# A two-layer hybrid decoder step on one core: a new deal of the adaLN pieces, and a start by feature tile

## The chip, the cores and the metric

The kernel runs on one core of a Trainium2 chip. The metric is device time in microseconds (us): the median of repeated executions of the whole step, both layers, from one launch. Lower is better. Engines are named as in the profile: PE (TensorE, matrix multiplication), PEld (its weight loads), DVE (VectorE), ACT (ScalarE), POOL (GpSimd), SP (SyncE, which issues nearly all transfers).

## The reference, cut to what matters

Two layers, each of three sub-layers: SwiGLU FFN, token mixer, SwiGLU FFN. 256 prompt tokens and 8 sequences of 8 sampled tokens (320 columns in all) go through together; D_MODEL is 1024, D_FF 2816, everything is float32. Each sub-layer is wrapped in a norm before, a norm after and a shift, scale and gate that come from one vector per sequence:

```
mod = (silu(c) @ ada_w + ada_b).reshape(B, 3, 3, 1024)      # per layer: 9 chunks of 1024 columns

def modulate(y, i): return rms_norm(y, g_pre[i]) * (1.0 + mod[:, i, 1]) + mod[:, i, 0]
def residual(y, out, i, w): return y + w * mod[:, i, 2] * rms_norm(out, g_post[i])

x = residual(x, swiglu(modulate(x, 0), f_in[0], f_out[0]), 0, 0.5)
x = residual(x, mixer(modulate(x, 1), ...), 1, 1.0)
x = residual(x, swiglu(modulate(x, 2), f_in[1], f_out[1]), 2, 0.5)
```

The mixer is one input projection, then a gated linear recurrence (HGRN2), sliding-window attention with sinks and a short convolution side by side, and one output projection. The nine vectors of conditioning are 1 prompt and 8 samples. `ada_w` is 2 layers x 1024 x 9216 floats, 75 MB: a third of all weights.

## The kernel before, in words

**Layout.** Activations lie feature-first: `x`, `y`, `sq` are 8 feature tiles of 128 partitions x 320 columns. A weight unit of 1 MB (1.4 MB for an FFN's second matrix) lands in one of two slots of `raw`. ACT copies it, rounded, to `WHI` (L899), DVE writes the rest, raw minus WHI, to `WLO` (L1180). The normed input is split in the same way into `hmh` and `hml`. A product is three matmuls (mm3, L466 to L468), so a *pair* of 256 output features takes 2 x 8 x 3 = 48 matmuls. An iteration of FFN-in is two pairs: slot 0 makes the gate (PSUM banks 0 and 1), slot 1 the other half (banks 2 and 3). FFN-in has 11 iterations, FFN-out 4 (banks 4 and 5, then 0 and 1), the mixer's input projection 5, its output projection 2.

**The adaLN product** is cut into 72 pieces of 1 MB: 18 chunks (shift, scale or gate of one sub-layer) of 4 pieces. A piece is 128 partitions x 2048 floats; PE multiplies it in `columns` (L475, 8 matmuls of 256 columns, which the trace counts as 16). When a chunk's four pieces are summed in its PSUM bank (6 or 7), ACT copies the bank to `adp` (`ada_copy`, L904), PE turns it (`turned`, L492) and DVE adds the bias (`mod_out`, L1195). The first two chunks, shift and scale of the first norm, come before all else, in buffers `first` (L214); the other 64 pieces are dealt out by the list `HOMES` to places in PE's program, and each has a *home*: the tile `ada`, or a part of `stage`, which lies over the normed operands and the FFN's intermediate (homes S, B, C), over `z` and `big` of the mixer (P), or over the idle normed operands (M). A home is loaded again only when its last piece has been multiplied: SP waits for `s_part` in `piece` (L364).

**What sets the order.** Everything is written out by hand; each engine runs its own list and waits on semaphores. PE takes one piece per iteration of the first FFN-in. A norm gap (`gap`, L590) is: statistics of the sub-layer's output (`y_stats`, L528 and L530), five pieces, statistics of the new x (`x_stats`, L522), three pieces, and then the first pair of the next sub-layer with k outside, as the feature tiles of the normed input come. Meanwhile ACT and DVE do: reciprocal root, y scaled and added to x, x squared (L924), reciprocal root, `x_norm` (DVE L1221 and L1242, ACT L935 and L938). In the mixer, PE runs six Gram groups (L655, each in one of two bank pairs), and DVE masks (L1409) and sums (L1413) each; DVE then scales the states (L1428), scores come (L684), and the recurrence's output (L700, L703) needs the states. Layer 0 has 12 pieces in its mixer, layer 1 has 8: one after each Gram group, and the rest between later steps.

**At the start**, SP issues small inputs, x, seven pieces, waits for a home and issues the eighth, then two weight units. PE does x_stats, the eight pieces and the turns; DVE then makes the whole scale (L1211) and the norm runs over the tiles, while PE multiplies the first pair with k outside and the second with k inside.

**The states' and caches' outputs** leave in ten transfers that ACT issues between the mixer and its output projection (L1130 to L1140).

Of the kernel before, what the change touches and what calls it, by code (L numbers as in the profile page):

```python
# [16 lines left out]
F32 = mybir.dt.float32  # L17
# [36 lines left out]
START = 2  # L54
# [3 lines left out]
FFN_GAP = ["S0", "S1", "ada", "B0", "B1", "B2", "C0", "C1"]  # L58
MIX_GAP = ["ada", "M"]
OUT_GAP = ["P0", "P1", "P2", "ada", "S0", "S1", "P0", "ada"]  # L60
N_FIRST, N_MIX = 12, (12, 8)
HOMES = ["ada"] * N_FIRST + FFN_GAP + MIX_GAP * 6 + OUT_GAP + FFN_GAP + FFN_GAP + MIX_GAP * 4
LANDS = 12
# [5 lines left out]
         "C0": (HHL0 + 7040, HHL0 + 8064), "C1": (HHL0 + 9088, HHL0 + 10112),  # L69
         "P0": (Z0 + 2240, Z0 + 3264), "P1": (Z0 + 4288, Z0 + 5312), "P2": (BIG0, BIG0 + 1024)}  # L70
# [30 lines left out]
DVE_CHAIN = 57  # L101
# [50 lines left out]
def trunk(nc, A, O):  # L152

    ctx = ExitStack()
    with ctx:
# [35 lines left out]
        with ExitStack() as stage_scope:  # L191
# [22 lines left out]
                 yf[:, 0:2048], ada[:, :, :].rearrange("p a b -> p (a b)"), zfl[:, 0:2048]]  # L214
# [32 lines left out]
        def chunk_of(n, j):  # L247

            return START + 3 * n + j

# [10 lines left out]
        s_first = [sem(f"s_first{i}") for i in range(START * PIECES)]  # L261
# [5 lines left out]
        s_part = sem("s_part")  # L267
        s_adp = sem("s_adp")
# [44 lines left out]
        ADA = A["ada_w"].rearrange("l u p n -> (l u) p n")  # L313
# [35 lines left out]
        def _(sp):  # L349
# [5 lines left out]
            for u in range(START * PIECES):  # L355
                if u == START * PIECES - 1:
                    sp.wait_ge(s_part, 2)
                sp.dma_start(first[u], ADA[((DEPTH - 1) * CHUNKS + 7) * PIECES + u]).then_inc(s_first[u], 16)

            taken = {"ada": 6}  # L360

            def piece(p):

                u = START * PIECES + p  # L364
                if HOMES[p] in taken:
                    sp.wait_ge(s_part, taken[HOMES[p]] + 2)
                taken[HOMES[p]] = u
# [8 lines left out]

            def ffn_in(l, f, off):
# [4 lines left out]
                both(0)  # L382
                n = 3 * l + 2 * f
                if n == 0:
                    piece(0)
                    for it in range(1, IT_IN):
                        piece(it)
                        both(it)
                    piece(N_FIRST - 1)
                else:  # L390
                    if n == 2:
                        sp.wait_ge(s_used[1], l * ITS + OFF_MO + IT_MO + 1)
                        for p in range(36, 40):
                            piece(p)
                    if n == 3:
                        last = (l - 1) * ITS + OFF_F1O + IT_OUT - 1
                        free_ffn(last, 40)
# [4 lines left out]
            def free_ffn(last, p0):  # L402
# [5 lines left out]
                piece(p0 + 6)  # L408
                piece(p0 + 7)
# [10 lines left out]
            for l in range(DEPTH):  # L420
                ffn_in(l, 0, OFF_F0I)
                gap = 12 if l == 0 else 48
                ffn_out(l, 0, OFF_F0O, gap)
                for it in range(IT_MI):
                    for slot in (0, 1):
                        weights(l * ITS + OFF_MI + it, slot, MIN_[l * 2 * IT_MI + it * 2 + slot], W_IN)
                    if it == 0:
                        free_ffn(l * ITS + OFF_F0O + IT_OUT - 1, gap)

                        sp.wait_ge(s_part, START * PIECES + gap + 9)  # L430
# [3 lines left out]
                mix = gap + 8  # L434
                for it in range(IT_MO):
                    for slot in (0, 1):
                        weights(l * ITS + OFF_MO + it, slot, MOUT[l * 2 * IT_MO + it * 2 + slot], W_IN)
                    if it == 0:
                        piece(mix)
                        sp.wait_ge(s_used[1], l * ITS + OFF_MI + IT_MI + 1)  # L440
                        for p in range(mix + 1, mix + 4):
                            piece(p)
                for p in range(mix + 4, mix + N_MIX[l]):
                    piece(p)
                if l == 0:

                    sp.wait_ge(ev["mixl"], 4 * (l + 1))
                    for p in range(32, 36):
                        piece(p)
                ffn_in(l, 1, OFF_F1I)  # L450
                ffn_out(l, 1, OFF_F1O, 40 if l == 0 else None)
# [8 lines left out]
        def _(pe):  # L460
# [18 lines left out]
            def partial(p):  # L479

                u = START * PIECES + p
                c = u // PIECES
# [1313 lines left out]
```

## Time and profile before

| | us |
|---|---|
| median of 3 runs | 1445.57 (1443.24 to 1445.70) |
| profiled execution | 1445.13 |
| its span, first to last instruction | 1443.3 |
| PE busy | 1347.7 (93%) |
| DVE busy | 689.8 (48%) |
| ACT busy | 558.2 (39%) |
| POOL busy | 86.4 (6%) |
| read from HBM | 249.26 MB, 176 GB/s over the span |
| mean granted TensorE clock | 0.972 |

The 1.8 us between the profiled execution's time and its span lie outside the instructions. PE is busy for 1347.7 of 1443.3 us, so what is left to win on waits is under 96 us; the profile's second part shows where PE is not at nine or ten tenths: in the first slice, and in three groups of slices, about 280 to 320 us, 380 to 510 us and 1080 to 1200 us. These are the start, the norm gaps and the two mixers.

### The profile page before, as it was taken

Reading aid. Unit: us, or ns where it says so; the run is one execution under the profiler, and the core shown is the slowest. Engines: PE = TensorE matmul, PEld = TensorE weight load, DVE = VectorE, ACT = ScalarE, POOL = GpSimd, SP = SyncE. Lnnn points to the kernel's source line nnn. Section 1 sums busy time; section 2 is a strip of 40 time slices with the busy share of each in tenths; the row PEclk is TensorE's granted clock in tenths of the full one; section 3 lists DMA queues with packets and bytes.
Section 4 is the critical chain, followed back from the end, with each engine's and each line's share of the span. In section 5 each row is a group of like instructions: output and inputs, shape, how many; then the busy total and the mean of one; then the engine's idle time right before and its main releaser. Section 6 shows DMA issues by size and latency. Waiting matters only on the chain.

```text
span 1443.3 us, 23409 instructions
## 1 busy us (share of the span) xinstructions
PE 1347.7 (93%) x10190; PEld 1256.6 (87%) x10190; DVE 689.8 (48%) x715; ACT 558.2 (39%) x703; POOL 86.4 (6%) x93
## 2 busy tenths in 40 slices
PE   4899999999877999999999999999996888999997
PEld 2799999979744889999989999997994678999997
DVE  0534443358644544444344444435686545444433
ACT  2533343354313553333345333425351445333331
POOL 0000000001611000000000000000035100000000
PEclk9899999999979999999999999999999899999999
DMA  9655656454652744446462344745547042444440
GB/s 362 241 205 203 210 204 246 160 219 146 229 210 94 264 159 147 145 146 248 162 251 99 146 148 151 272 156 196 190 157 264 3 136 88 151 150 163 163 161 37
DMA packets 50372, 255.42 MB, mean 177 GB/s; under 512 B 7022, under 2 KB 12014, under 8 KB 30062
## 3 DMA queue, kind: packets, MB, share of 16 engines
q1 hardware_dynamic: 45872, 249.51, 47.5%
q10 hardware_dynamic: 4238, 3.58, 0.8%
q8 instruction: 67, 1.10, 0.3%
q0 software_dynamic: 176, 1.09, 0.2%
q14 instruction: 19, 0.16, 0.0%
HBM read 249.26 MB, written 4.89 MB: 176 GB/s over the span
## 4 chain that ended last, share of the span: by engine, by line
PE 84%; ACT 6%; DMA 5%; DVE 3%; ACTq 1%; issue 1%; SPq 0%; DVEq 0%
PE PS L466 25%; PE PS L467 25%; PE PS L468 25%; DMA ada<-in_ada_w 3%; PE PS L475 3%; PE PS L522 2%; ACT hmh L935 2%; ACT sq L935 2%; DMA raw<-in_w_in 1%; DMA x<-in_x 1%; PE PS L716 0%; ACT big L1043 0%; PE PS L700 0%; PE PS L616 0%; PE PS L789 0%
## 5 line engine op out<-in xcount | busy, mean ns | idle before, releaser
L466 PE MATMUL PS<-hmh,WHI 128*128 128x320 f32 x1856 | 578.9, 312 | 12.9 <-DVE hml L1242 11.8
L467 PE MATMUL PS<-hml,WHI 128*128 128x320 f32 x1856 | 572.9, 309 | 0.0
L468 PE MATMUL PS<-hmh,WLO 128*128 128x320 f32 x1856 | 572.7, 309 | 0.0
L1180 DVE TENSOR_TENSOR WLO<-raw,WHI 128x2048 fp32r<-128x2048 f32 (+1 forms) x148 | 366.2, 2474 | 390.1 <-ACT WHI L899 390.1
L899 ACT ACTIVATE WHI<-raw 128x2048 fp32r<-128x2048 f32 (+1 forms) x148 | 303.9, 2053 | 346.2 <-PE PS L468 346.1
L466 PEld LDWEIGHTS PS<-hmh,WHI 128*128 128x128 f32 x1856 | 349.4, 188 | 26.1 <-issue 14.7
L467 PEld LDWEIGHTS PS<-hml,WHI 128*128 128x128 f32 x1856 | 349.6, 188 | 0.2
L468 PEld LDWEIGHTS PS<-hmh,WLO 128*128 128x128 f32 x1856 | 349.4, 188 | 0.0
L466 PE MATMUL PS<-hhl,WHI 128*128 128x320 f32 x704 | 216.8, 308 | 0.0
L468 PE MATMUL PS<-hhl,WLO 128*128 128x320 f32 x704 | 216.7, 308 | 0.0
L467 PE MATMUL PS<-hhl,WHI 128*128 128x320 f32 x704 | 216.7, 308 | 0.0
L467 PEld LDWEIGHTS PS<-hhl,WHI 128*128 128x128 f32 x704 | 132.0, 188 | 0.0
L466 PEld LDWEIGHTS PS<-hhl,WHI 128*128 128x128 f32 x704 | 132.0, 188 | 0.0
L468 PEld LDWEIGHTS PS<-hhl,WLO 128*128 128x128 f32 x704 | 132.0, 188 | 0.0
L973 ACT ACTIVATE y<-PS 128x640 f32<-128x640 f32 x44 | 31.0, 705 | 182.7 <-PE PS L468 182.7
L1297 DVE TENSOR_TENSOR y<-y,PS 128x640 f32<-128x640 f32 x44 | 36.1, 821 | 106.1 <-PE PS L468 106.1
L475 PE MATMUL PS<-ada,cT 128*32 128x256 f32 x448 | 34.4, 430 | 28.6 <-DMA ada<-in_ada_w 28.6
L954 ACT ACTIVATE sq<-PS 128x640 f32<-128x640 f32 x18 | 12.7, 705 | 101.7 <-PE PS L468 101.7
L1285 DVE TENSOR_TENSOR acc<-acc,sq 128x320 f32<-128x320 f32 x18 | 8.9, 494 | 83.3 <-ACT sq L954 66.7
L475 PEld LDWEIGHTS PS<-ada,cT 128*32 128x32 f32 x448 | 13.4, 117 | 40.1 <-issue 20.7
L522 PE MATMUL PS<-sq,cst 128*128 128x320 f32 x96 | 32.3, 493 | 15.3 <-ACT sq L1085 11.1
L475 PE MATMUL PS<-stage,cT 128*32 128x256 f32 x592 | 37.9, 392 | 7.5 <-DMA stage<-in_ada_w 7.4
(227 smaller groups left out, 879.7 us busy)
## 6 DMA issues: line engine op xcount, KB each, us to landing
raw<-in_w_in SPq DMA_DIRECT2D x88, 1024.0 KB, 4.7
raw<-in_w_out SPq DMA_DIRECT2D x32, 1408.0 KB, 6.0
stage<-in_ada_w SPq DMA_DIRECT2D x74, 512.0 KB, 6.8
ada<-in_ada_w SPq DMA_DIRECT2D x54, 512.0 KB, 6.0
raw<-in_m_in SPq DMA_DIRECT2D x20, 1024.0 KB, 4.8
raw<-in_m_out SPq DMA_DIRECT2D x8, 1024.0 KB, 6.5
z<-in_ada_w SPq DMA_DIRECT2D x4, 1024.0 KB, 11.9
big<-in_ada_w SPq DMA_DIRECT2D x2, 1024.0 KB, 15.8
```

The costliest lines, as they stand in the source:

```text
L466: mm(out, hi, rhi, start=first, stop=False)
L467: mm(out, hi, rlo, start=False, stop=False)
L468: return mm(out, lo, rhi, start=False, stop=last)
L475: last = mm(PS[32 * j:32 * j + 32, bank, 0:256], cT[:, k, :], halves[i][:, j * 256:(j + 1) * 256], start=(k == 0), stop=(k == KT - 1))
L522: last = mm(PS[:, 5, 0:T], ones, sq[:, k, :], start=(k == 0), stop=(k == KT - 1))
L899: a_(WHI[:, slot, 0:width], raw[:, slot, 0:width], ACT.Copy).then_inc(s_hi[slot], 1)
L935: a_(out[:, k, 0:TP], sq[:, k, 0:TP], ACT.Identity, bias=mod[m][:, 8 + k, 0:1], scale=mod[m][:, 16 + k, 0:1])
L954: a_(sq[:, 0:2, :], PS[:, bank:bank + 2, 0:T], ACT.Square).then_inc(s_sqd, 1)
L973: a_(sg, PS[:, 0:2, 0:T], ACT.Silu).then_inc(s_gread, 1)
L1180: tt(WLO[:, slot, 0:width], raw[:, slot, 0:width], WHI[:, slot, 0:width].bitcast(F32), ALU.subtract).then_inc(s_lo[slot], 1)
L1285: ch.link(tt(acc[:], acc[:], sq[:, 0, :], ALU.add))
L1297: tt(hf, sg, PS[:, 2:4, 0:T], ALU.mult).then_inc(s_uread, 1)
```

## The change: what it does

1. **The deal.** Of the 64 pieces that are dealt, twelve still go to the first FFN-in (two ahead of its second iteration, and then one each). Each of the four full norm gaps takes ten instead of eight: seven between `y_stats` and `x_stats` instead of five, and three behind as before. Each mixer takes six, instead of twelve and eight: one ahead, one after Gram groups 2, 4 and 6, and one at each of two later places. New homes are C2 and P3.
2. **Banks.** Chunks lie in bank 4, 6 or 7 by the table `BANKS`. So that bank 4 and 5 are free, FFN-out uses banks 0 to 3 (its first iteration waits for `s_gread`, its second for `s_uread`), and all `y_stats` go to bank 5. One more wait (`s_mod`) stands ahead of a turn in the mixer's input projection.
3. **The start.** The first shift and scale are laid out anew on the host (`ada0`): a piece holds all 1024 inputs for one feature tile's 128 shifts and 128 scales. PE makes one feature tile's shift and scale from one piece; ACT copies, PE turns by two small matmuls (9 columns each), DVE adds the bias, makes the scale, and the norm of that feature tile follows. Both first pairs run with k outside. SP issues the eight pieces without a wait, with the first two weight units behind pieces 0 and 1.
4. **Outputs.** The ten output transfers of a layer are issued by SP, ahead of the second FFN's weights, and no longer by ACT.
5. **Norms.** In `x_norm` of DVE the two small operations on a tile's samples now follow one another with a link between them, instead of being interleaved over two tiles; and one turn moves from the output projection's first to its second iteration.

```diff
-FFN_GAP = ["S0", "S1", "ada", "B0", "B1", "B2", "C0", "C1"]
-OUT_GAP = ["P0", "P1", "P2", "ada", "S0", "S1", "P0", "ada"]
-N_FIRST, N_MIX = 12, (12, 8)
+FFN_GAP = ["S0", "S1", "ada", "B0", "B1", "B2", "C0", "C1", "C2", "ada"]
+MIX_GAP = ["ada", "M"] * 3
+OUT_GAP = ["P0", "P1", "P2", "P3", "ada", "S0", "S1", "P0", "P1", "ada"]
...
+            taken = {}
+            for k in range(KT):
+                sp.dma_start(first[k], A["ada0"][k]).then_inc(s_first[k], 16)
+                if k < 2:
+                    weights(0, k, WIN_[k], W_IN)
...
                 y_stats(n, 5)
-                for i in range(5):
+                for i in range(7):
                     partial(p + i)
                 x_stats(n + 1)
-                for i in range(5, 8):
+                for i in range(7, 10):
                     partial(p + i)
...
                         last.then_inc(ev["gr"], 1)
                         n += 1
-                        partial(p + n)
+                        if n % 2 == 0:
+                            partial(p + n // 2)
...
+            for k in range(KT):                       # PE
+                pe.wait_ge(s_first[k], 16)
+                if k > 1:
+                    pe.wait_ge(s_m0, k - 1)
...
+                last.then_inc(s_p0, 1)
+                if k:
+                    started(0, k - 1)
+                pe.wait_ge(s_a0, k + 1)
...
+                last.then_inc(s_t0, 1)
+                if k > 2:
+                    started(1, k - 3)
+            started(0, KT - 1)
+            for k in range(KT - 3, KT):
+                started(1, k)
...
+            for k in range(KT):                       # ACT
+                act.wait_ge(s_p0, k + 1)
+                if k > 1:
+                    act.wait_ge(s_t0, k - 1)
+                a_(adps[k % 2], PS[:, 6 + k % 2, 0:256], ACT.Copy).then_inc(s_a0, 1)
+                act.wait_ge(s_mt, k + 1)
+                act.wait_ge(s_m0, k + 1)
+                feed(k, 2, k, k + 1)
+                if k < 2:
+                    hi_split(k, 0, W_IN)
...
+                for k in range(KT):                   # DVE, first_norm; all eight normed(k) stand ahead
+                    dve.wait_ge(s_t0, k + 1)
...
+                        ALU.add, ALU.mult).then_inc(s_m0, 1)
+                    dve.wait_ge(s_m0, k + 1)
+                    shifted(k, 2, k, k + 1)
+                    low(k, k, k + 1)
+                    if k < 2:
+                        lo_split(k, 0, W_IN)
```

`started(slot, k)` is the six matmuls of tile k of a pair; for k = 0 it also waits for both halves of that slot's weights. `feed` is the loop body of ACT's old `x_norm`. The `#` remarks behind loops are added here.

**PE at the start.** Before: x_stats, eight pieces (x24 is three of them, x16 two), the two turns (L492), piece 0 of the deal (`ada`), and the first pair.

```order
L522 MATMUL PS<-sq,cst 128x320 x8
L475 MATMUL PS<-z,cT 32x256 x24
L475 MATMUL PS<-big,cT 32x256 x16
L492 MATMUL PS<-cst,adp 128x128 x2
L475 MATMUL PS<-y,cT 32x256 x8
L475 MATMUL PS<-ada,cT 32x256 x8
L475 MATMUL PS<-z,cT 32x256 x8
L492 MATMUL PS<-cst,y 128x128 x2
L475 MATMUL PS<-ada,cT 32x256 x8
L466 MATMUL PS<-hmh,WHI 128x320
```

And now, where L852 is a piece, L859 the turn of one tile and L492 to L494 the three matmuls of a product:

```order
L547 MATMUL PS<-sq,cst 128x320 x8
L852 MATMUL PS<-z,cT 32x256 x8
L859 MATMUL PS<-cst,adp 128x9 x2
L852 MATMUL PS<-z,cT 32x256 x8
L492 MATMUL PS<-hmh,WHI 128x320
L493 MATMUL PS<-hml,WHI 128x320
L494 MATMUL PS<-hmh,WLO 128x320
L492 MATMUL PS<-hmh,WHI 128x320
L493 MATMUL PS<-hml,WHI 128x320
L494 MATMUL PS<-hmh,WLO 128x320
L859 MATMUL PS<-cst,y 128x9 x2
L852 MATMUL PS<-z,cT 32x256 x8
```

The first products now stand behind two pieces instead of nine, but the second turn stands behind the first tile's six matmuls.

**PE in layer 0's mixer.** Before, from the second Gram group (L655) on, with a piece (L475) behind each group and L668 the states:

```order
L655 MATMUL PS<-big 64x64 x12
L475 MATMUL PS<-ada,cT 32x256 x8
L668 MATMUL PS<-sq 128x128 x8
L655 MATMUL PS<-big 64x64 x6
L655 MATMUL PS<-z,y 64x64 x2
L475 MATMUL PS<-stage,cT 32x256 x8
L655 MATMUL PS<-big 64x64 x12
L655 MATMUL PS<-z,y 64x64 x4
L655 MATMUL PS<-big 64x64 x12
L475 MATMUL PS<-ada,cT 32x256 x8
```

Now, with L680 for the Gram groups, L501 for a piece and L694 for the states:

```order
L680 MATMUL PS<-big 64x64 x12
L501 MATMUL PS<-stage,cT 32x256 x8
L694 MATMUL PS<-sq 128x128 x8
L680 MATMUL PS<-big 64x64 x6
L680 MATMUL PS<-z,y 64x64 x2
L680 MATMUL PS<-big 64x64 x12
L680 MATMUL PS<-z,y 64x64 x4
L680 MATMUL PS<-big 64x64 x12
L501 MATMUL PS<-ada,cT 32x256 x8
```

Behind the states three Gram groups now follow one another up to the next piece. The homes alternate, so a home comes up again four groups after its last use; before, it was two.

## Rows read from the trace of the kernel before

**Rows 1.** Busy time by stretch (both mixers' Gram parts, both output projections):

```profile
382.76:422.81 40.05, 24.38 (x429) 14.67 (x425) 22.06 (x39) 4.34 (x6) 15.38 (x18) 0.79 0.85 307
1086.01:1116.72 30.71, 18.66 (x396) 12.73 (x393) 20.68 (x38) 4.35 (x6) 15.36 (x18) 0.89 0.83 309
459.21:493.42 34.21, 30.47 (x199) 30.21 (x198) 11.64 (x16) 12.24 (x23) 1.23 (x3) 0.95 0.69 238
1152.29:1181.89 29.60, 28.71 (x197) 28.45 (x195) 11.51 (x15) 11.85 (x22) 1.23 (x3) 1.00 0.40 133
```

**Rows 2.** Timeline, layer 0's mixer: start us, length us, engine, operation, [idle before]:

```profile
387.23 1.16 DVE L1409 TENSOR_TENSOR raw<-PS,cst 128x448 f32<-128x448 f32 x2 [0.76 <-POOL z L1674]
389.94 1.14 DVE L1409 TENSOR_TENSOR raw<-PS,cst 128x448 f32<-128x448 f32 x2
...
403.13 1.94 PE L475 MATMUL PS<-ada,cT 128*32 128x256 f32 x16 [4.81 <-DMA ada<-in_ada_w]
422.81 0.45 PE L703 MATMUL PS<-sq 64*64 64x64 f32 x8
```

**Rows 3.** Timeline, layer 1's mixer:

```profile
1090.48 1.16 DVE L1409 TENSOR_TENSOR raw<-PS,cst 128x448 f32<-128x448 f32 x2 [0.76 <-POOL z L1674]
...
1111.36 0.74 DVE L1409 TENSOR_TENSOR raw<-PS,cst 64x256 f32<-64x256 f32 x2
1112.03 1.14 DVE L1413 TENSOR_REDUCE sq<-raw 64x64 f32<-64x256 f32 x2
...
1116.72 0.45 PE L703 MATMUL PS<-sq 64*64 64x64 f32 x8 [1.64 <-DVE raw L1428]
```

**Rows 4.** Timeline, layer 0's output projection (ACT's queue and PE):

```profile
467.60 2.11 ACTq L1140 DMA_DIRECT2D out_conv<-cso  x1
...
470.25 0.60 PE L492 MATMUL PS<-cst,adp 128*128 128x128 f32 x2 [3.74 <-ACT adp L904]
```

**Rows 5.** The chain that ended last, first norm gap: start us, us, what:

```profile
291.65 4.45 PE PS L475 x80
296.10 4.78 PE PS L522 x16
```

**Rows 6.** Timeline, the same gap (ACT) and the gap behind layer 0's mixer (PE):

```profile
297.65 1.62 ACT L924 ACTIVATE sq<-x 128x640 f32<-128x640 f32 x3 [0.40 <-DVE x L1276]
...
498.99 1.07 PE L475 MATMUL PS<-stage,cT 128*32 128x256 f32 x16 [0.48 <-DMA stage<-in_ada_w]
```

**Rows 7.** Timeline, the start: landings, and the end of the first two pairs:

```profile
18.77 0.47 ACT L1089 ACTIVATE rst<-rt 128x320 f32<-128x320 f32 x1
...
22.88 1.07 PE L475 MATMUL PS<-big,cT 128*32 128x256 f32 x16 [1.02 <-DMA big<-in_ada_w]
...
25.37 1.07 PE L475 MATMUL PS<-y,cT 128*32 128x256 f32 x16 [1.05 <-DMA y<-in_ada_w]
...
52.71 0.31 PE L466 MATMUL PS<-hmh,WHI 128*128 128x320 f32 x1
...
59.51 0.82 DVE L1297 TENSOR_TENSOR y<-y,PS 128x640 f32<-128x640 f32 x1 [3.60 <-PE PS L468]
```

**Rows 8.** Timeline, the start: the operations of which the new loop is made:

```profile
21.93 0.38 ACT L1092 ACTIVATE adp<-PS 128x256 f32<-128x256 f32 x1 [2.68 <-PE PS L475]
...
34.35 1.91 ACT L899 ACTIVATE WHI<-raw 128x2048 fp32r<-128x2048 f32 x1
35.05 0.23 DVE L1195 TENSOR_TENSOR modC<-PS,par 128x72 f32<-128x72 f32 x1 [10.39 <-PE PS L492]
...
36.36 2.29 DVE L1180 TENSOR_TENSOR WLO<-raw,WHI 128x2048 fp32r<-128x2048 f32 x1 [0.40 <-ACT WHI L899]
38.57 0.89 DVE L1221 TENSOR_TENSOR sq<-x,rst 128x320 f32<-128x320 f32 x2
39.09 0.60 ACT L935 ACTIVATE hmh<-sq,modC 128x256 fp32r<-128x256 f32 x1 [2.83 <-DVE sq L1221]
...
41.28 0.62 PE L466 MATMUL PS<-hmh,WHI 128*128 128x320 f32 x1
```

More of the change, by code:

```diff
@@ L354, in _ @@
             sp.dma_start(x[:], A["x"]).then_inc(s_xin, 16)
[L355 to L360, printed above, removed]
             def piece(p):
-                u = START * PIECES + p
                 if HOMES[p] in taken:
                     sp.wait_ge(s_part, taken[HOMES[p]] + 2)
-                taken[HOMES[p]] = u
+                taken[HOMES[p]] = p
                 for half in (0, 1):
@@ L407, in free_ffn @@
                 sp.wait_ge(s_used[1], last + 2)
-                piece(p0 + 6)
-                piece(p0 + 7)
+                for p in range(p0 + 6, p0 + 10):
+                    piece(p)
             def ffn_out(l, f, off, p0):
@@ L479, in partial @@
             def partial(p):
-                u = START * PIECES + p
-                c = u // PIECES
-                if u % PIECES == 0:
-                    pe.wait_ge(s_mod, c)
+                c = p // PIECES
+                if p % PIECES == 0 and BANKS[c] in BANKS[:c]:
+                    pe.wait_ge(s_mod, max(i for i in range(c) if BANKS[i] == BANKS[c]) + 2)
                 pe.wait_ge(s_ada[p % LANDS], 32 * (p // LANDS + 1))
-                columns(u, 6 + c % 2, home(p))
+                columns(p, BANKS[c], home(p))
             def turned(c, adp=adp):
@@ L571, in ffn_out @@
                     g = l * ITS + off + it
-                    bank = 0 if it % 2 else 4
+                    bank = 2 * (it % 2)
+                    if it == 0:
+                        pe.wait_ge(s_gread, (2 * l + f + 1) * IT_IN + 1)
                     if it == 1:
-                        pe.wait_ge(s_gread, (2 * l + f + 1) * IT_IN + 1)
+                        pe.wait_ge(s_uread, (2 * l + f + 1) * IT_IN + 1)
                     if it > 1:
@@ L588, in ffn_out, with gap @@
                         last.then_inc(s_used[slot], 1)
-            def gap(n, bank, p):
+            def gap(n, p):
                 if p is None:
-                    y_stats(n, bank)
+                    y_stats(n, 5)
                     if n < 3 * DEPTH - 1:
@@ L837, in _ @@
                         pe.wait_ge(s_pr, 3 * l + 1)
+                        pe.wait_ge(s_mod, done + 2)
                         turn(lambda a: z[:, Z_I + a, :], 4, ev["itp"])
@@ L925, in x_rms, with feed @@
                 rms(5, rst[:], s_r, 1.0 / D, s_xst, n + 1)
+            def feed(done, m, a, b):
+                for out in (hmh, sq):
+                    for k in range(a, b):
+                        a_(out[:, k, 0:TP], sq[:, k, 0:TP], ACT.Identity, bias=mod[m][:, 8 + k, 0:1],
+                           scale=mod[m][:, 16 + k, 0:1])
+                act.wait_ge(s_ms, done + 1)
+                a_(hmh[:, a:b, TP:T], sq[:, a:b, TP:T], ACT.Copy).then_inc(s_hmh, 1)
             def x_norm(n, m, staged=None):
                 if staged is not None:
[L930 removed]
+                    act.wait_ge(s_part, staged + 2)
                 for i, (a, b) in enumerate(FEEDS):
[L932 to L938 removed]
+                    act.wait_ge(s_mt, fed(n) + i + 1)
+                    feed(fed(n) + i, m, a, b)
             def y_norm(n, bank):
@@ L1238, in low @@
[L1238 to L1250 removed]
+                normed(*FEEDS[0])
```

326 lines of the change are left out of this document (152 added, 174 removed).

## The prediction

> **What bounds the kernel now.** I read the shares of busy time first: PE is busy for 93% of the span, so the time is PE's work plus the stretches in which PE waits or runs at half clock. The chain that ended last and the waits by engine say where these are, and the busy time by stretch puts numbers on those that this change touches. In the Gram parts of the two mixers, 40.05 and 30.71 us, PE is busy for 24.38 and 18.66 us at a granted clock of 0.79 and 0.89 [rows 1]. Inside, the same pattern comes again: a Gram group, then PE stands for a piece of the adaLN weights, 4.81 us in the worst case [rows 2]; DVE, which has to mask and sum each group, stands for PE. So the transfers set the pace, with a DMA share of 0.85 and 0.83 [rows 1]. In the output projections PE waits for an ACT that is issuing output transfers [rows 4]. In a norm gap, pieces and statistics follow one another on PE with no wait [rows 5]. The start is one chain of landings, then norm [rows 7].
>
> **Mixers.** With a piece behind every second group only, the next bound is DVE, which can't start before 387.23 in either version (it waits for POOL, and neither POOL's work nor what is ahead of it changes). A full group costs DVE 389.94 - 387.23 = 2.71 us [rows 2], a half one 1112.03 + 1.14 - 1111.36 = 1.81 us [rows 3]. Four full and two half groups: 14.46 us. Then the states are scaled, and from the last sum's end to the recurrence's output (L703) it is 1116.72 - 1113.17 = 3.55 us [rows 3]. So L703 comes 18.0 us after DVE's start: at 405.2 instead of 422.81 in layer 0, **-17.6 us** [rows 2], at 1108.5 instead of 1116.72 in layer 1, **-8.2 us** [rows 3]. Does PE keep up? Each group has to be there before DVE wants it, and with two bank pairs PE may be a group ahead. The piece behind group 4 is the first on a home (`ada`) that is freed only as this part begins, at 382.76, the start of the first stretch of [rows 1]; DVE wants group 5, the one behind it, at 387.23 + 3 x 2.71 + 1.81 = 397.2. That leaves 14.4 us for a transfer of 1 MB, where landings come 2.49 us apart when the queue is full [rows 7]. I take no wait here. The pieces at the two later places cost nothing: layer 1 had one fewer place there than layer 0, and DVE's chain is what ends last.
>
> **Outputs.** ACT's queue issues ten transfers until 467.60 + 2.11 = 469.71, and only then copies the bank that PE turns: PE stands for 3.74 us [rows 4], and its clock is halved behind the pause (0.95 over 34.21 us is 3.4 us at half clock [rows 1]). 192 matmuls at 0.147 us (from 52.71, the fourth of 48, to the end near 59.4 [rows 7]) and the turn make 28.5 us; the stretches take 34.21 and 29.60 us [rows 1]: **-5.7 and -1.1 us**. On SP, the issues lie between the mixer's end and the second FFN's first weights, whose slot is free only after the split in the output projection; I cost that at nothing. If SP were late, ACT would stand in its weight copy ahead of the squares; 2 us at most.
>
> **Norm gaps.** 80 piece matmuls take 4.45 us, 0.89 us a piece, and x_stats follows at once and takes 4.78 us [rows 5]. ACT's last squares end at 297.65 + 1.62 = 299.27 [rows 6], x_stats at 300.88: it is bound by PE already, so two more pieces ahead of it push the norm by their whole 1.78 us. Three such gaps (layer 0 and 1 before the mixers, and between the layers): **+5.4 us**. The gap behind layer 0's mixer is different: S0, loaded only when the last pair is done, is there at 498.99 and x_stats starts at 499.99 [rows 6]. Now S1 has to be there too: 2.49 us later, if landings are as far apart as 22.88 and 25.37 [rows 7], so x_stats starts at 502.4: **+2.4 us**. The three pieces behind x_stats stay hidden behind the norm.
>
> **Start.** Before, the two first pairs are done at 59.4 (DVE's wait for them ends at 59.51 [rows 7]), the next iteration's operands are ready, and PE goes on. Now the loop has these terms. The reciprocal root is there at 18.77 + 0.47 = 19.24 [rows 7]. DVE norms all eight tiles, 0.89 us for two [rows 8]: 22.8. Bias and scale are two operations of 0.23 us (the rows' forms are larger; I take 0.5 us with handoffs) [rows 8]. From ACT's first hmh to the first matmul it is 41.28 - 39.09 = 2.2 us [rows 8]. But for tiles 0 and 1 the weights' split stands in the way: ACT's feed 1.3, copy to WHI 1.91, DVE's WLO 2.29 [rows 8]. Tile 0: 22.8 + 0.5 + 1.3 + 1.9 + 2.3 = 28.8. PE has then stood for some 7 us and starts at half clock: six matmuls 1.7, the second turn 0.5, so 31.0. Tile 1: + 0.5 + 1.3 + 1.9 + 2.3 = 37.0. Tile 2: + 0.5 + 2.2 = 39.7, six matmuls at half clock and the turn: 41.8 is the turn of tile 3. From then on a tile costs one round: turn done, 0.5 + 2.2 us, six matmuls 0.9 us, next turn 0.3 us = 3.9 us, while PE's own work in it at full clock is a piece (1.07 [rows 7]), twelve matmuls (1.8) and the turn, 3.2 us. Tile 7's turn is done at 41.8 + 4 x 3.9 = 57.4, the first pair at 57.4 + 2.7 + 0.9 = 61.0. Behind it, ACT reads the gate (0.7), copies WHI (1.9), DVE writes WLO (2.3): 65.9 for the second iteration's start; PE's three left tiles of the second pair (2.7) and the two pieces ahead of that iteration (2.1) end at 65.8. Against 59.2: **+6.7 us**. Ends: with full clock throughout and a round of 3.5 us it is +3; with half clock it is +14 (below). The landings don't bind: ten transfers 2.49 us apart behind x have all landed near 25.37 + 4 x 2.49 = 35.3 [rows 7], 22 us ahead of tile 7's turn. What this start buys is early matmuls; what it pays is a round trip through three engines for each tile where one norm ran in a pipeline.
>
> The Trainium skill speaks against this start: its page "TensorE: Matmul & The Clock Gate", section "HAM oscillation — how this bites in real kernels", says that bursts of matmuls with waits between them leave the clock low for each burst, and that only sustained work releases it. By that rule all of the loop would run at 1.2 GHz. The trace has both: 0.79 and 0.89 in the Gram parts with PE busy for 61% of the time, but 0.95 to 1.00 in the output projections with 89 to 97% [rows 1]. At half clock PE would be busy without a pause in the loop, so I expect it to rise.
>
> **Other edits.** The banks, the waits for `s_gread` and `s_uread` (their readers have a whole pair, 48 x 0.147 = 7 us, or a whole iteration), the later turn, the linked sample operations (ACT's feed is the longer of the two): nothing, because PE's pair or ACT covers each; a few tenths of a us where that cover is gone.
>
> **Sum.** -17.6 - 8.2 - 5.7 - 1.1 + 5.4 + 2.4 + 6.7 = -18.1 us. The profiled execution took 1445.13 us, so 1427.0; the median is 0.4 us above it: **1427 us**.
>
> **Rivals.**
> *Half clock in the start.* A round is then PE's own work: piece 1.94 [rows 2], twelve matmuls 3.2, turn 0.5 = 5.6 us. Tile 7's turn at 41.8 + 4 x 5.6 = 64.2, first pair 68.5, second iteration 73.5: +14.3 instead of +6.7, so 1435. For it: the clock in the Gram parts. Against: PE would never pause.
> *The start follows the landings.* If the handoffs overlap better than I add them up, a tile costs 2.49 us [rows 7] and, from 31.0, the second iteration starts about 11 us sooner than I have it, near 55: 1416. Against: the second turn stands behind the first six matmuls, tile by tile.
> *The mixers stay bound by pieces.* If the piece behind group 4 or 6 comes late by the waits of now, half of the 25.8 us is lost: 1440. Against: half as many pieces in a stretch with a DMA share of 0.85.
> *Slower: the seventh piece in each gap.* Home C0 (S1 behind the mixer) is filled only once the last pair is done, and PE stands for it ahead of x_stats. C0 is asked for some 5.3 us after that (y_stats and six pieces), and S0 needed about that long in the gap behind the mixer. If it came as late as the mixer's pieces, 4.81 us [rows 2], with 1.7 us for a clock halved for 3.4 us [rows 1], in four gaps: +26, so 1453. From 4.5 us a gap on, the kernel is slower than before. For it: each gap loads 2 MB more. Against: the queue is empty then.
>
> **How the numbers follow.** Forecast 0.60 (1421 to 1433), half clock 0.17, landings 0.10, mixers bound by pieces 0.08, slower 0.05. 1416 to 1438 holds the forecast, nearly all of the half-clock case and part of the landings' case, some 0.82. A measurement of this kernel can tell 0.2% (2.9 us) from no change. Slower by more than that: 0.04; within it: 0.03, tails of the mixers' and the gap's case; faster: 0.93.
>
> **What would show it.** DVE's twelve masks in each mixer without idle time, and L703's counterpart at 18.0 us from the first; no PE wait for a turn in the output projections, and clock 1.00 there; x_stats 1.8 us later behind y_stats, without a DMA wait; in the start, tile turns 3.9 us apart from the fourth on, and the second iteration's first matmul near 66. I am wrong if the turns are 2.5 or 5.6 us apart, if PE waits for `ada` or `stage` between Gram groups, or if a seventh piece is waited for.

## The result: 4% slower, and where the time went

| | median of runs, us | ratio to before, 95% interval | profiled span, us | mean granted clock |
|---|---|---|---|---|
| before | 1445.63 (1443.24 to 1448.43, 4 runs) | | 1443.3 | 0.972 |
| changed | 1504.01 (1502.76 to 1507.19, 4 runs) | 1.0406 (1.0381 to 1.0432) | 1505.4 | 0.951 |

The forecast was 1427 us, range 1416 to 1438. The loss is one piece of the program, and it is not one that the forecast had put a price on. Both traces, cut at the same landmarks, give this ledger (change of the distance between two landmarks, us):

| stretch | forecast | measured |
|---|---|---|
| start, to the second iteration's first matmul | +6.7 | +6.5 |
| rest of the first FFN, to the end of its y_stats | 0 | **+64.2** |
| gap 1, to the end of x_stats | +1.8 | +1.5 |
| layer 0: VectorE's first mask to the recurrence's output | -17.6 | -17.6 |
| layer 0: from there through the output projection | -5.7 | -1.2 |
| gap behind it | +2.4 | +3.7 |
| the two other gaps with pieces | +3.6 | +5.2 |
| layer 1: VectorE's first mask to the recurrence's output | -8.2 | -8.3 |
| layer 1: from there through the output projection | -1.1 | +5.0 |
| the last gap and FFN | 0 | +3.1 |
| sum | -18.1 | +62.1 |

The busy time by stretch shows it at once. Columns as in [rows 1]: stretch and length, busy us (and count) of PE, PEld, DVE, ACT, POOL, then PE's clock, the DMA share and GB/s. The first FFN-in before:

```profile
59.20:204.00 144.80, 144.80 (x1061) 137.87 (x1061) 59.40 (x41) 48.51 (x40) 0.00 (x0) 1.00 0.59 210
```

and after:

```profile
65.70:204.00 138.30, 108.22 (x704) 99.74 (x705) 39.60 (x27) 31.76 (x27) 0.00 (x0) 0.89 0.40 145
```

PE goes from never idle to 30.1 us idle in 138.3, and the DMA share falls from 0.59 to 0.40. That speaks against a lack of bandwidth and for something that is asked for late. The waits by engine name it (us in total, times, longest). Before, seven of ten were in the mixers, two at the start and one in a gap; none stood in the first FFN-in from its second iteration on:

```profile
PE PS L475 <- DMA ada<-in_ada_w: 28.6, 10, 4.8
```

After, nine of the eleven, all but 0.7 us of the time, are in the first FFN-in, one an iteration:

```profile
PE PS L501 <- DMA ada<-in_ada_w: 46.3, 11, 5.5
```

Two pieces of the timeline, 22 us apart:

```profile
77.22 1.07 PE L501 MATMUL PS<-ada,cT 128*32 128x256 f32 x16 [4.23 <-DMA ada<-in_ada_w]
...
99.06 1.51 PE L501 MATMUL PS<-ada,cT 128*32 128x256 f32 x12 [4.98 <-DMA ada<-in_ada_w]
```

An iteration took 15.3 us before. Up to y_stats PE does the same matmuls in 250.3 us of busy time that took 231.6 before, and it is idle for 45.6 us besides: 18.6 and 45.6 make the 64.2. The 18.6 are slower matmuls behind the waits; from 78.20 to 81.50 us, for example, the granted clock is 0.50. The chain that ended last, in order of time (start us, us, what), says why it is 22 now:

```profile
66.34 2.21 DVE WLO L1215
68.61 0.33 SPq L376
68.99 0.42 SPq L370
69.47 7.70 DMA ada<-in_ada_w
77.22 1.07 PE PS L501 x16
```

L370 is `piece`, L376 is `weights` (L369 and L375 in the kernel before). SP issues in program order. Its load of slot 1's weights waits for VectorE's WLO of slot 1 (L1215, ending 68.55), and the piece, whose home `ada` had been free since PE was done with piece 0 at 64.4, stands behind that load. SP's own queue, before:

```profile
67.57 1.60 SPq L369 DMA_DIRECT2D ada<-in_ada_w  x2
71.45 8.03 SPq L375 DMA_DIRECT2D raw<-in_w_in  x2
82.84 0.80 SPq L369 DMA_DIRECT2D ada<-in_ada_w  x2
```

and after:

```profile
65.68 3.26 SPq L376 DMA_DIRECT2D raw<-in_w_in  x2
68.99 0.90 SPq L370 DMA_DIRECT2D ada<-in_ada_w  x2
77.92 13.87 SPq L376 DMA_DIRECT2D raw<-in_w_in  x2
91.84 0.90 SPq L370 DMA_DIRECT2D ada<-in_ada_w  x2
```

The 13.87 us are two loads merged, the second waiting for its slot. It is the loop that matters. PE multiplies a piece between slot 0's pair and slot 1's pair; WLO of slot 1 needs slot 1's pair done; the next piece needs that WLO. So piece, pair, WHI, WLO, issue and transfer stand in one ring: from 77.22 to 99.06 it is 9.9 us on PE to ACT's WHI (at 87.14), 2.0 to DVE's WLO (89.09), 2.75 to the piece's issue (91.84) and 7.2 for the transfer, 21.8 us. Before, a piece stood ahead of its iteration's two loads: at 82.84 the loads of the iteration before had been issued 3.4 us earlier, and the piece waited for its home alone.

**The rest of the trace after.** The two mixers did just what was worked out: VectorE goes without a pause from 459.41 and 1152.73, and the output comes 17.99 and 17.96 us later (forecast 18.0; before [rows 2, 3]).

```profile
459.41 1.15 DVE L1449 TENSOR_TENSOR raw<-PS,cst 128x448 f32<-128x448 f32 x2 [0.75 <-POOL z L1706]
...
477.40 0.76 PE L726 MATMUL PS<-sq 64*64 64x64 f32 x8 [1.81 <-DVE raw L1468]
...
1152.73 1.16 DVE L1449 TENSOR_TENSOR raw<-PS,cst 128x448 f32<-128x448 f32 x2 [0.75 <-POOL z L1706]
...
1170.69 0.69 PE L726 MATMUL PS<-sq 64*64 64x64 f32 x8 [1.41 <-DVE raw L1468]
```

The start too: the turns of tiles 4 to 7 come 3.83 us apart (forecast 3.9), the last at 56.76, done at 57.27 (57.4), and the second iteration starts at 65.71 (66).

```profile
45.28 0.51 PE L859 MATMUL PS<-cst,adp 128*128 128x9 f32 x4
...
56.76 0.51 PE L859 MATMUL PS<-cst,y 128*128 128x9 f32 x4
...
65.71 0.39 PE L492 MATMUL PS<-hmh,WHI 128*128 128x320 f32 x1 [0.47 <-issue]
```

In layer 0's output projection PE's wait for the turn [rows 4] is gone, but SP comes late with the next FFN's weights: the issue of `out_vp` alone takes 6.58 us of SP's queue, ACT stands 4.35 us for `raw`, and behind it everything up to y_stats. PE is busy for 28.67 us of this projection's 32.30, near the 28.5 forecast; the wait of 3.63 us ahead of y_stats comes on top.

```profile
524.74 6.58 SPq L472 DMA_DIRECT2D out_vp<-big  x1
...
534.75 0.85 SPq L376 DMA_DIRECT2D raw<-in_w_in  x2
```

```profile
541.85 1.91 ACT L941 ACTIVATE WHI<-raw 128x2048 fp32r<-128x2048 f32 x1 [4.35 <-DMA raw<-in_w_in]
...
546.76 1.44 PE L553 MATMUL PS<-acc,cst 128*128 128x320 f32 x2 [3.63 <-DVE acc L1323]
```

The norm gaps carry two pieces more, as in the chain of the first one, to be read against [rows 5]; in two of the four PE waits for the seventh piece, 1.26 us and 0.38 us, far from the 4.5 us from which the slower rival would have decided:

```profile
362.38 6.18 PE PS L501 x112
368.56 4.52 PE PS L547 x16
```

```profile
808.73 1.07 PE L501 MATMUL PS<-stage,cT 128*32 128x256 f32 x16 [1.26 <-DMA stage<-in_ada_w]
```

Layer 1 loses 4.1 us between the recurrence and the output projection. There PE works at a lower clock than before: the first 17.3 us behind the recurrence's output run at half clock, where 0.65 and 0.74 were granted before. There is also a piece more. Before, then after:

```profile
1116.70:1124.00 7.30, 7.28 (x90) 6.24 (x91) 4.78 (x7) 1.59 (x6) 0.00 (x0) 0.65 0.01 2
1124.00:1134.00 10.00, 9.75 (x139) 6.46 (x137) 5.19 (x9) 7.40 (x32) 6.04 (x6) 0.74 0.01 2
```

```profile
1170.70:1178.00 7.30, 7.30 (x63) 5.89 (x65) 4.75 (x7) 0.18 (x1) 0.00 (x0) 0.50 0.06 11
1178.00:1188.00 10.00, 9.90 (x97) 6.77 (x98) 4.77 (x7) 7.41 (x31) 6.04 (x6) 0.52 0.01 2
```

### The profile page after: what moved, and what is told of

The parts are those of the page before. It is cut to its first block, busy times and chain, and to the rows that moved or that the text cites. A ratio compares the mean times of both kernels' runs of the same rounds, so it can differ in the third digit from the quotient of the medians.

```text
span 1505.4 us, 23507 instructions
## 1 busy us (share of the span) xinstructions
PE 1374.9 (91%) x10218; PEld 1279.7 (85%) x10218; DVE 694.2 (46%) x740; ACT 561.2 (37%) x712; POOL 86.9 (6%) x93
## 4 chain that ended last, share of the span: by engine, by line
PE 75%; ACT 6%; DVE 6%; DMA 6%; issue 2%; POOL 2%; SPq 2%; DVEq 0%; ACTq 0%; POOLq 0%
PE PS L492 23%; PE PS L493 22%; PE PS L494 22%; DMA ada<-in_ada_w 4%; PE PS L501 2%; PE PS L547 2%; DVE WLO L1215 2%; ACT WHI L941 2%; ACT hmh L973 1%; ACT sq L973 1%; DMA stage<-in_ada_w 1%; DVE raw L1449 1%; POOL y L1713 1%; SPq L370 1%; DVE sq L1453 1%
## 5 line engine op out<-in xcount | busy, mean ns | idle before, releaser
L492 PE MATMUL PS<-hmh,WHI 128*128 128x320 f32 x1856 | 586.7, 316 | 25.7 <-DVE hml L1263 17.6
L493 PE MATMUL PS<-hml,WHI 128*128 128x320 f32 x1856 | 578.7, 312 | 0.0
L494 PE MATMUL PS<-hmh,WLO 128*128 128x320 f32 x1856 | 578.1, 311 | 0.0
L1215 DVE TENSOR_TENSOR WLO<-raw,WHI 128x2048 fp32r<-128x2048 f32 (+1 forms) x148 | 366.1, 2474 | 400.5 <-ACT WHI L941 400.5
L492 PEld LDWEIGHTS PS<-hmh,WHI 128*128 128x128 f32 x1856 | 355.2, 191 | 44.0 <-issue 26.2
L493 PEld LDWEIGHTS PS<-hml,WHI 128*128 128x128 f32 x1856 | 355.7, 192 | 0.2
L494 PEld LDWEIGHTS PS<-hmh,WLO 128*128 128x128 f32 x1856 | 354.7, 191 | 0.0
L492 PE MATMUL PS<-hhl,WHI 128*128 128x320 f32 x704 | 216.8, 308 | 0.0
L494 PE MATMUL PS<-hhl,WLO 128*128 128x320 f32 x704 | 216.7, 308 | 0.0
L494 PEld LDWEIGHTS PS<-hhl,WLO 128*128 128x128 f32 x704 | 132.0, 188 | 0.0
L492 PEld LDWEIGHTS PS<-hhl,WHI 128*128 128x128 f32 x704 | 132.0, 187 | 0.0
L501 PE MATMUL PS<-ada,cT 128*32 128x256 f32 x400 | 35.3, 483 | 46.4 <-DMA ada<-in_ada_w 46.3
L501 PEld LDWEIGHTS PS<-ada,cT 128*32 128x32 f32 x400 | 12.7, 128 | 60.6 <-DMA ada<-in_ada_w 45.0
L501 PE MATMUL PS<-stage,cT 128*32 128x256 f32 x624 | 40.2, 394 | 6.7 <-DMA stage<-in_ada_w 4.2
```

The lines of the kernel that those rows point to most:

```text
L492: mm(out, hi, rhi, start=first, stop=False)
L493: mm(out, hi, rlo, start=False, stop=False)
L494: return mm(out, lo, rhi, start=False, stop=last)
L501: last = mm(PS[32 * j:32 * j + 32, bank, 0:256], cT[:, k, :], halves[i][:, j * 256:(j + 1) * 256], start=(k == 0), stop=(k == KT - 1))
L1215: tt(WLO[:, slot, 0:width], raw[:, slot, 0:width], WHI[:, slot, 0:width].bitcast(F32), ALU.subtract).then_inc(s_lo[slot], 1)
```

## The experiments

Each ran on one of four chips beside the kernel before, whose medians there were 1446.09 (experiments 1, 2, 3, 5), 1447.44 (4, 6, 7, 8), 1447.52 (9, 10) and 1446.43 (11). Medians are in us, ratios are to the kernel before on the same chip, with 95% intervals. Experiments on different chips are better compared by their ratios.

**1. The order alone, put back.** In the changed kernel:

```diff
                     for it in range(2, IT_IN):
-                        both(it)
                         piece(it)
+                        both(it)
```

> The changed kernel with one thing put back: from the third iteration of the first FFN-in on, SP again issues a piece ahead of the two weight loads, not behind them. My theory (the piece stands in SP's queue behind slot 1's weights, which wait for WLO; TensorE then waits 4 to 5.5 us for the piece in each iteration and runs at half clock behind it): iterations return from 22.3 us to about 15.3, nine of them give back 60 to 64 us, and the kernel takes 1440 to 1444 us; the windows of this stretch show TensorE busy throughout at clock 1.00. Rival (the feature-tile start with its new homes and k outside leaves TensorE cold, and the order matters little): at most 15 us come back, 1489 or more.

Measured: 1437.89 (1432.24 to 1441.1), ratio 0.9937 (0.9915 to 0.9958). 66 us come back (2 us more than the range expected), and the stretch has no idle time and full clock:

```profile
66.00:210.00 144.00, 144.00 (x1055) 137.06 (x1055) 58.94 (x41) 46.71 (x39) 0.00 (x0) 1.00 0.62 215
```

So the exchange of two lines is the whole loss; the rest of the change is a gain of 0.6%.

**2. The exchange alone, in the kernel before.**

```diff
                     for it in range(1, IT_IN):
-                        piece(it)
                         both(it)
+                        piece(it)
```

> The kernel before with the one swap alone: in the first FFN-in each piece from piece 1 on is issued behind both weight loads of its iteration. My theory: the swap alone costs what it costs in the changed kernel, ten iterations of +6 to +7 us, 1505 to 1515 us, with waits of TensorE for ada of 4 to 5.5 us. Rival (the swap costs only in company with the new start): 1446 to 1460 us.

Measured: 1518.66 (one run), 73 us above 1446.09, the median of the kernel before on that chip. It needs no new start to cost what it costs. The waits of TensorE for `ada` are 81.9 us in 20 places, against 28.6 in 10. It came 4 us above the range expected: the ring is closed from the second iteration here, and the last matmul of its y_stats starts 75.7 us behind that of the kernel before (366.57 against 290.84), 7.6 us for each of ten pieces. From there to the end the two traces take nearly the same time (1150.3 and 1152.5 us), so the single run's loss lies all in this stretch.

**3. More homes, same order.**

```diff
-HOMES = ["ada", "C0"] + ["ada"] * (N_FIRST - 2) + ...
+HOMES = ["ada", "C0"] + ["C1", "C2", "C0", "C1", "C2"] + ["ada"] * 5 + ...
```

> The changed kernel with its order of issue, but pieces 2 to 6 land in C1, C2, C0, C1, C2 in place of ada, so that no piece of these has to wait until the piece before it has been used. My theory (the place in SP's queue is the bound, not the home): 1501 to 1507 us, waits of TensorE for these pieces unchanged at 4 to 5.5 us. Rival (the round trip through the single home is the bound): five iterations of about 15.3 us in place of 22.3, some 30 us less, 1472 us.

Measured: 1499.1 (one run), 2 us below the range expected and 5 us below the changed kernel. Five pieces are on homes that have long been free, and PE waits for each as before, 4.10 to 5.37 us:

```profile
77.84 1.93 PE L501 MATMUL PS<-stage,cT 128*32 128x256 f32 x16 [4.10 <-DMA stage<-in_ada_w]
100.45 1.91 PE L501 MATMUL PS<-stage,cT 128*32 128x256 f32 x16 [4.71 <-DMA stage<-in_ada_w]
```

The round trip through one buffer is not the cause, since that rival would have brought 30 us. With experiments 1 and 4, what is left is the place in SP's queue.

**4. Which of the two loads?** The piece goes between them:

```diff
                     for it in range(2, IT_IN):
-                        both(it)
+                        weights(l * ITS + off + it, 0, WIN_[...], W_IN)
                         piece(it)
+                        weights(l * ITS + off + it, 1, WIN_[...], W_IN)
```

> The changed kernel with one place moved: in the first FFN-in, from the third iteration on, SP issues slot 0's weights, then the piece, then slot 1's weights. My theory (what delays the piece is the wait of slot 1's weight load for WLO of slot 1, some 7 us later than slot 0's): the waits of TensorE for ada go, and the time is that of the kernel with the piece ahead of both, 1435 to 1445 us. Rival (any weight load ahead of the piece delays it, by its wait for WLO or by the 1 MB in front of it in the DMA queue): a wait of 2 us or more in each of nine iterations stays, 1460 us or more.

Measured: 1438.59 (one run), that of experiment 1 within 1 us. PE is busy for 143.10 of the 144.00 us at clock 1.00. A load ahead of the piece costs nothing; only the one that waits for slot 1's WLO does.

**5. The old start, with the order put back.** The text on record describes this kernel wrongly in one point: its first FFN-in has the piece ahead of the weights, as in experiment 1, not the order of the changed kernel. It is therefore to be compared with experiment 1, and its expected times don't apply. The start is that of the kernel before: two chunks of four pieces, one norm, both slots of the first pair with k inside. The diff is against experiment 1; the same start in the lists of PE, ACT and DVE and in the host's layout is left out.

```diff
-HOMES = ["ada", "C0"] + ["ada"] * (N_FIRST - 2) + ...
+HOMES = ["ada"] * N_FIRST + ...
...
-                    both(1)
+                    both(0)
                     sp.wait_ge(s_p0, 7)
                     piece(0)
-                    sp.wait_ge(s_p0, 8)
-                    piece(1)
-                    for it in range(2, IT_IN):
+                    for it in range(1, IT_IN):
                         piece(it)
                         both(it)
...
-                    for it in range(1, IT_IN):
-                        if it == 1:
-                            partial(1)
-                        body(it, ...)
+                    for it in range(IT_IN):
+                        body(it, ...)
```

> The changed kernel with its order of issue in the first FFN-in as it is, but with the start of the kernel before: two chunks of four pieces by input rows, one whole norm, both slots of the first pair with k inside, one ada home for the first twelve pieces. Since pieces here go behind the weights only from the second iteration on, as in the changed kernel, the slow iterations stay (and there is one more of them). My theory: the start gives back its 6.5 us and the piece of the second iteration, now on ada behind the weights or not, changes it by up to 7 us the other way: 1495 to 1507 us. Rival (the new start causes the loss in the iterations): 1440 us.

Measured: 1427.9 (1426.01 to 1433.45), ratio 0.9868 (0.9829 to 0.9907), on the chip of experiment 1. The new start costs 10 us by the medians; in the traces the last matmul of y_stats starts at 297.4 with it and at 289.4 without, and at 290.8 in the kernel before: 6.6 to 8.0, where 6.7 was forecast.

**6. The outputs off SP's queue.** To experiment 5:

```diff
-                sp.wait_ge(ev["cv"], l + 1)
-                ...
-                sp.dma_start(O["conv"][l], cso[:]).then_inc(s_out, 16)
...
                 last.then_inc(ev["sd"], 1)
+                pool.wait_ge(ev["cv"], l + 1)
+                ...
+                pool.dma_start(O["conv"][l], cso[:]).then_inc(s_po, 16)
                 gates(3 * l + 1, 1, range(4))
```

> Compared with the version that has the piece ahead of the weights and the old start (1427.9 us): the outputs of a mixer go from SP's queue to GpSimd's, behind its last work in the mixer. Theory: in layer 0 SP no longer stands 12 us at the outputs (out_vp alone 6.84 us), so the weights of the next FFN-in are on chip before ScalarE needs them (it waited 1.60 us for raw) and the pieces of the gap are issued earlier (TensorE waited 2.53 us for one): 2 to 4 us less, 1424 to 1426 us. Rival (the DMA engines are full in this stretch, share 1.02, so that who issues is of no account): 1427 to 1429 us.

Measured: 1429.58 (1425.41 to 1432.67), ratio 0.9878 (0.9847 to 0.991): no difference from experiment 5 that the intervals can tell. In the traces, layer 0's y_stats comes 3.1 us earlier (its last matmul at 472.72 against 475.85). ACT no longer waits for `raw` (1.60 us in experiment 5) nor PE for VectorE's sum (0.81 us), as the theory has it. But PE still waits for the seventh piece of the gap, 2.75 us against 2.53: that half of the theory fell, and the medians show no gain.

**7. The gap's pieces, five and five.** To experiment 5:

```diff
-                for i in range(7):
+                for i in range(5):
                     partial(p + i)
                 x_stats(n + 1)
-                for i in range(7, 10):
+                for i in range(5, 10):
                     partial(p + i)
```

> Compared with the version that has the piece ahead of the weights and the old start (1427.9 us): of the ten pieces of a norm gap five, not seven, stand ahead of the statistics of x, and five behind. Theory (TensorE's work in a gap is ten pieces and the statistics, some 10 + 4.6 us, longer than the norm beside it; with seven ahead, the norm that waits for the statistics comes on top): 1 us a gap in three gaps and 3.5 us in the second one, where TensorE waits 2.53 us for a piece in front of the statistics: 1421 to 1424 us. Rival (five pieces behind the statistics delay the first pair by what they free): 1427 to 1429 us.

Measured: 1423.92 (1422.59 to 1424.7), ratio 0.9834 (0.9815 to 0.9852), 4 us below experiment 5 by the medians, 5 by the ratios; the intervals overlap. The gap behind layer 0's mixer shows what goes. In experiment 5 the seventh piece is waited for, and then x_stats runs at a granted clock of 0.73:

```profile
484.40 1.07 PE L496 MATMUL PS<-stage,cT 128*32 128x256 f32 x16 [2.53 <-DMA stage<-in_ada_w]
485.40 6.27 PE L542 MATMUL PS<-sq,cst 128*128 128x320 f32 x16
```

With five ahead, at a clock of 1.00:

```profile
480.08 4.57 PE L542 MATMUL PS<-sq,cst 128*128 128x320 f32 x16
484.58 3.66 PE L496 MATMUL PS<-stage,cT 128*32 128x256 f32 x64
```

**8. Experiments 6 and 7 together,** both diffs.

> Both edits together: the outputs on GpSimd's queue and the gap's pieces split five and five, with the piece ahead of the weights and the old start. Theory: the gains add in part, since both remove the wait of 2.53 us in the second gap: 1419 to 1423 us. Rival: no better than the better of the two alone.

Measured: 1419.74 (1416.62 to 1425.29), ratio 0.9799 (0.9772 to 0.9826). It is 1.9% below the 1447.44 that the kernel before took on that chip, and the interval lies below that of experiment 5.

**9. Six and four.** To experiment 8:

```diff
-                for i in range(5):
+                for i in range(6):
...
-                for i in range(5, 10):
+                for i in range(6, 10):
```

> The version with outputs on GpSimd's queue, old start and the piece ahead of the weights, its gaps split six and four in place of five and five (1419.7 us). Theory (TensorE is never idle in a gap with either split, its ten pieces and the statistics fill it): the same within 2 us, 1418 to 1422 us. Rival (the sixth piece ahead of the statistics delays them, as the sixth and seventh did): 3 us or more behind, 1423 us or more.

Measured: 1418.58 (1416.17 to 1419.85), ratio 0.9806 (0.9774 to 0.9838): the same as five and five. These two are the fastest of the study, and nothing here tells them apart.

**10. Was it TensorE's work that bound the mixers?** To experiment 7, with the three pieces beside the Gram matrices computed again, twice more in layer 0 and once more in layer 1 (the second argument; the sums then come out wrong):

```diff
                         if n % 2 == 0:
-                            partial(p + n // 2)
+                            partial(p + n // 2, 2 - l)
```

> Compared with the version with the old start, the piece ahead of the weights and five and five pieces in a gap (1423.9 us): beside the Gram matrices each of the three pieces is computed three times in layer 0 and twice in layer 1 (the modulations that come of them are wrong), so that TensorE has 3 x 3 + 1 = 10 and 2 x 3 + 1 = 7 pieces there, where the kernel before had 9 and 7; no transfer is added. Theory (before, TensorE's pieces bound this part of the mixer; now VectorE does): the gains of 17.6 and 8.2 us go, 20 to 30 us in all, 1444 to 1454 us. Rival (the gain came from the order or from the transfers that went, not from TensorE's work): under 8 us, 1432 us at most.

Measured: 1421.59 (1418.79 to 1422.79), ratio 0.9826 (0.9794 to 0.9858): no cost that the runs can tell. This theory fell. Layer 0, where 48 matmuls stand in place of 16 behind each of three groups (the second row is the piece behind the fourth), has its output 18.59 us after VectorE's start instead of 18.01:

```profile
385.91 1.16 DVE L1425 TENSOR_TENSOR raw<-PS,cst 128x448 f32<-128x448 f32 x2 [0.75 <-POOL z L1682]
...
404.50 0.45 PE L724 MATMUL PS<-sq 64*64 64x64 f32 x8 [0.79 <-DVE raw L1444]
```

```profile
392.60 2.80 PE L496 MATMUL PS<-ada,cT 128*32 128x256 f32 x48
```

From VectorE's start to the output the granted clock is 1.00 here, in both layers, against 0.82 and 0.85 in experiment 7, so a faster clock paid for part of the added work: PE is busy for 15.1 us of layer 0's 18.6, against 11.6 of 18.0.

**11. Or their transfers?** To experiment 7, with these three pieces fetched twice, one after the other, into their homes:

```diff
+                m = [q for l in range(DEPTH) for q in range(AT_MIX[l] + 1, AT_MIX[l] + 4)]
+                if p in m:
+                    for half in (0, 1):
+                        sp.dma_start(home(p)[half], ADA[p, ...]).then_inc(s_dup, 16)
+                    sp.wait_ge(s_dup, 32 * (m.index(p) + 1))
                 for half in (0, 1):
                     sp.dma_start(home(p)[half], ADA[p, ...]).then_inc(s_ada[p % LANDS], 16)
```

> Compared with the version with the old start, the piece ahead of the weights and five and five pieces in a gap (1423.9 us): beside the Gram matrices each of the three pieces is fetched twice in a row into its home, SP waiting for the first copy, so that a piece's round trip is two transfers of 1 MB; TensorE's work is as it was. Theory (before, the round trips of the pieces through two homes set the pace of this part, not TensorE's matmuls, which were added again without cost): waits of TensorE for these pieces come back, and 12 to 20 us of the mixers' 25.8, 1434 to 1444 us. Rival (the gain of the new deal has nothing to do with transfers either): under 4 us, 1428 us at most.

Measured: 1436.48 (1434.84 to 1443.92), ratio 0.9941 (0.9925 to 0.9957): 12.6 us more by the medians, 15.5 by the ratios. The picture of [rows 2] is back, PE standing for a piece and DVE for PE:

```profile
390.90 1.94 PE L502 MATMUL PS<-stage,cT 128*32 128x256 f32 x16 [6.25 <-DMA stage<-in_ada_w]
```

```profile
386.44 1.16 DVE L1427 TENSOR_TENSOR raw<-PS,cst 128x448 f32<-128x448 f32 x2 [0.75 <-POOL z L1684]
...
395.94 0.75 DVE L1427 TENSOR_TENSOR raw<-PS,cst 64x256 f32<-64x256 f32 x2 [3.96 <-PE PS L680]
```

The output comes 26.7 us after VectorE's start in layer 0 (413.16) and 25.7 in layer 1 (1081.42 to 1107.07), against 18.0: 16.3 us of the 25.8 that the change had brought. Experiments 10 and 11 together say that most of the mixers' gain came from pieces that are no longer fetched there.

## Why the prediction was wrong

**The step that failed** is the list of costs that "Other edits" closes with "nothing, because PE's pair or ACT covers each". It names banks, waits, a turn and sample operations, but not the exchange of `piece(it)` and `both(it)` on SP. That exchange is in the kernel's diff; the sum has no term for it, and so puts the rest of the first FFN-in at 0 without a reason. What the runs showed in its place: +64.2 us in the trace, 66 us back by undoing it (experiment 1), 73 us by doing it alone (experiment 2). Spread over the nine iterations that wait, the 64.2 us are some 7.1 us each, of which 5.07 are PE's wait and 2.07 slower matmuls behind it. The trace before held the numbers to see it ahead: the two loads of an iteration take 8.03 us of SP's queue together, because the second waits for slot 1's WLO, and a transfer of a piece takes some 7 us more (7.70 in the chain above).

**Right**: both Gram parts, to 0.1 us, with the cause named (transfers set the pace, then VectorE); experiment 11 confirms the cause, and experiment 10, whose expectation had put TensorE's matmuls in the transfers' place, refutes that version of it. Also the start (+6.7 forecast, +6.5 in the trace, 3.83 us a tile), so neither start rival held. The clock rose in the loop, PE being busy for 86% and then 91% of it:

```profile
30.00:45.00 15.00, 12.93 (x86) 9.11 (x85) 6.06 (x16) 6.43 (x13) 0.00 (x0) 0.64 0.61 240
45.00:57.00 12.00, 10.93 (x102) 8.39 (x102) 3.86 (x15) 4.86 (x12) 0.00 (x0) 1.00 0.31 97
```

The prediction had read a rule into the Trainium skill's page "TensorE: Matmul & The Clock Gate", section "HAM oscillation — how this bites in real kernels", by which the whole loop would run at 1.2 GHz. That section tells of bursts that are shorter than the DMA waits between them. The loop was no such case: from 45 to 57 us no wait of PE was longer than 0.36 us, and the stretch stands at 2.4 GHz. No turn was waited for in the output projections. The slower rival named the wrong place: the longest wait for a seventh piece was 1.26 us.

**Mis-sized terms**, 16 us together. *Outputs on SP*: "2 us at most" was 3.6 us at y_stats (PE's wait for VectorE's sum, 546.76), and the -5.7 became -1.2. *Layer 1 behind the recurrence*: forecast without a term, +4.1 us by half clock and one more piece, and 0.9 more in the projection (clock 0.93, not 1.00). That the piece "costs nothing" is not borne out there, but its share was not told apart from the clock's, and what lowered the clock was not tested. *Gaps*: 10.4 for 7.8, the rest being short waits for homes and, behind the mixer, a lower clock (0.80). *The end*: forecast at 0, +3.1 us. x_stats of the last gap took 7.45 us where it took 6.06 before, behind the same wait of 4.19 us, and the FFN behind it took 1.7 us more; the cause was not tested. Without the exchange the same deal reaches 1437.89. That lies just inside the stated range, but 11 us above the forecast of 1427, so the other terms together were too hopeful.

## What to carry to other kernels

On a queue that issues in order, a load's wait belongs to everything behind it: for each two issues that a diff exchanges, ask what the earlier one waits for, and whether that hangs on the data of the later one; if so, the exchange closes a ring whose round trip becomes the loop's period. Price every moved line, the one-line ones too, from the queue's own timeline. And a buffer that is free says nothing of when it is filled: here more buffers changed next to nothing (1499.1 against 1504.01 us).

## What the runs showed of the hardware

The issue of one small output (`out_vp`, 64 KB) took 6.58 us on SP's queue in layer 0, and 0.71 us in layer 1 of the same trace (6.84 and 0.72 us in experiment 5). In layer 0, SP had issued five pieces of 1 MB in the 9 us ahead of it, from 515.63 on, and then five other outputs; in layer 1 it had issued neither weights nor pieces in the 26 us ahead. The DMA share alone does not tell the two apart: it is 1.01 during the long issue and 1.00 from 1193 to 1195 us, around the short one. What the long issue waited for is not shown.

Three times the piece matmuls beside layer 0's Gram matrices, and twice in layer 1, cost nothing that the medians can tell, and the clock granted there rose from 0.82 and 0.85 to 1.00 (experiments 7 and 10). In the gap behind layer 0's mixer, x_stats took 6.27 us at a clock of 0.73 behind a wait of 2.53 us, and 4.57 us at full clock without a wait (experiments 5 and 7). Behind the shorter wait of 1.26 us in the changed kernel it took 4.58 us: there the idle time was not paid for again.
